# State-space loop: two of the four turned products of each block move from VectorE to GpSimd

## The reference, cut to what matters

```python
def _s5_mixer(h, ...):
    bu_re = einsum('bsgc,gpc->bsgp', u, bb_re)     # the inputs of the states
    bu_im = einsum('bsgc,gpc->bsgp', u, bb_im)
    h_re, h_im = scan over s of  h = a * h + bu    # complex, 64 groups x 64 states
    y = (einsum('bsgp,gcp->bsgc', h_re, c_re) - einsum('bsgp,gcp->bsgc', h_im, c_im) + d * u)
    act = gelu(y)
    zg = act @ glu_w + glu_b
    return zg[..., :D_MODEL] * sigmoid(zg[..., D_MODEL:])
```

## Time and profile before

| | |
|---|---|
| median of 3 runs | 878.67 us (875.8 to 879.58) |
| the profiled execution | 876.96 us, of which the span of the profile is 875.2 us |
| TensorE busy | 804.0 us, 92% of the span |
| VectorE busy | 326.0 us, 37% |
| GpSimd busy | 183.1 us, 21% |
| ScalarE busy | 189.6 us, 22% |
| the state-space loop | from about 435 to 506 us of the span |

### The profile page before, as it was taken

The page is one execution under the profiler, slowest core; times in us unless marked ns, Lnnn a source line. Parts: engine busy times, 40 slices in busy tenths (PEclk is TensorE's granted clock), DMA queues, the critical chain, the costliest instruction groups (busy, mean ns, idle before and its releaser), DMA issues.

```text
span 875.2 us, 12777 instructions
## 1 busy us (share of the span) xinstructions
PE 804.0 (92%) x5191; PEld 449.3 (51%) x5192; DVE 326.0 (37%) x740; ACT 189.6 (22%) x315; POOL 183.1 (21%) x285
## 2 busy tenths in 40 slices
PE   3899979999999999999679999769999999989894
PEld 1367634565465565554555554434444756535441
DVE  1437994461131131311599711342000313214224
ACT  2402330351231221311700110421001203101112
POOL 2518679029400000000123200040011112101000
PEclk9999999999999999999979999869999999999998
DMA  9999999949999999994997792502788799999992
GB/s 322 347 357 387 382 369 342 345 158 422 420 421 422 422 423 422 422 420 204 363 372 264 259 382 97 192 17 100 294 318 304 274 422 417 419 420 420 418 401 76
DMA packets 72263, 289.66 MB, mean 331 GB/s; under 512 B 9302, under 2 KB 10614, under 8 KB 47384
## 3 DMA queue, kind: packets, MB, share of 16 engines
q1 hardware_dynamic: 66784, 279.98, 82.0%
q0 software_dynamic: 4736, 7.35, 2.5%
q10 hardware_dynamic: 696, 1.68, 0.5%
HBM read 281.64 MB, written 13.63 MB: 337 GB/s over the span
## 4 chain that ended last, share of the span: by engine, by line
PE 80%; DMA 9%; DVE 7%; SPq 2%; ACT 1%; issue 1%; DVEq 0%; ACTq 0%
PE PS L1876 20%; PE PS L1897 13%; PE PS L1905 7%; PE PS L2247 7%; PE PS L1879 6%; DMA ring<-in_moe_w 6%; PE PS L1929 4%; PE PS L1834 3%; PE PS L1608 3%; PE PS L1638 3%; DMA ring<-in_ab_w_in 2%; PE PS L1700 2%; PE PS L2232 2%; PE PS L1717 2%; SPq L392 2%; PE PS L2210 1%
## 5 line engine op out<-in xcount | busy, mean ns | idle before, releaser
L1897 PE MATMUL PS<-ring,work 128*64 128x512 f32 (+1 forms) x512 | 129.3, 595 | 2.6 <-DMA ring<-in_moe_w 2.5
L1876 PE MATMUL PS<-ring,hT 128*64 128x256 f32 x896 | 109.2, 386 | 7.4 <-DMA ring<-in_moe_w 7.4
L1876 PE MATMUL PS<-ring,yg 128*64 128x256 f32 x896 | 106.2, 379 | 0.0
L1425 DVE TENSOR_TENSOR work<-work,PS 128x512 f32<-128x512 f32 x32 | 22.0, 688 | 208.2 <-PE PS L1876 158.8
L1876 PEld LDWEIGHTS PS<-ring,hT 128*64 128x64 f32 x896 | 62.7, 138 | 49.1 <-issue 11.8
L1897 PEld LDWEIGHTS PS<-ring,work 128*64 128x64 f32 (+1 forms) x512 | 42.8, 143 | 76.0 <-issue 69.5
L1876 PEld LDWEIGHTS PS<-ring,yg 128*64 128x64 f32 x896 | 64.5, 137 | 32.6 <-issue 0.4
L1905 PE MATMUL PS<-work,xhat 128*128 128x256 f32 (+1 forms) x256 | 66.0, 417 | 4.0 <-issue 4.0
L682 POOL DMA_INDIRECT y_rows<-yg,row_no x24 | 23.4, 974 | 188.4 <-DVE yg L1433 164.9
L1905 PEld LDWEIGHTS PS<-work,xhat 128*128 128x128 f32 x256 | 48.9, 193 | 24.3 <-issue 18.3
L2247 PE MATMUL PS<-ring,yg 128*128 128x512 f32 x128 | 59.4, 615 | 0.0
(11 more groups left out here) (410 smaller groups left out, 1025.7 us busy)
## 6 DMA issues: line engine op xcount, KB each, us to landing
ring<-in_moe_w SPq DMA_DIRECT2D x96, 2048.0 KB, 16.0
ring<-in_ada_w SPq DMA_DIRECT2D x20, 2048.0 KB, 16.1
work<-in_ada_w SPq DMA_DIRECT2D x4, 2048.0 KB, 14.0
ring<-in_s_glu_w SPq DMA_DIRECT2D x4, 2048.0 KB, 11.8
ring<-in_ab_w_in SPq DMA_DIRECT2D x3, 2048.0 KB, 22.1
ring<-in_ab_w_out SPq DMA_DIRECT2D x2, 2048.0 KB, 15.4
ring<-rot_tables SPq DMA_DIRECT2D x2, 2048.0 KB, 11.2
rot_tables<-grow POOLq DMA_DIRECT2D x8, 256.0 KB, 5.6
```

Of the source, the lines that this page charges most:

```text
L1425: v.tensor_tensor(pairs_out(he[:, e % 2, :]), pairs_out(he[:, e % 2, :]), pairs(bank[e % 2 * 2 + 1 if direct else 1]), ALU.mult).then_inc( ...
L1876: last = mm(dst[64 * u:64 * u + 64, 0:256], hg[k][:, e * P:e * P + 64], w[:, k, 256 * u:256 * u + 256], start=k == 0, stop=k == KD - 1)
L1897: last = mm(dst, left[:, at:at + (64 if narrow else P)], w[:, c4, h * HALF:(h + 1) * HALF], start=c4 == 0, stop=c4 == KF - 1)
```

## The change

GpSimd makes products 0 and 3 of `turned(k)`, VectorE products 1 and 2, for every block. GpSimd's order becomes `turned(0)`, `sums(1)`, and then `sums(k + 1)`, `turned(k)`. The sums no longer wait for `q_ready` of the block before. All of GpSimd's steps in the loop count on one semaphore, `pool_s5`; `SUMMED(k)` and `TURNED(k)` are its values after the sums and the turned products of block `k`. `q_ready` now rises twice per block, after the scans and after VectorE's own products. In `products(k)` VectorE makes products 0 and 2 first and then waits for GpSimd's `turned(k - 2)`, whose operands products 1 and 3 overwrite. TensorE's `outputs(k)` and SP's two loads wait for both engines.

```diff
--- before.py
+++ after.py
@@ -67,6 +67,8 @@
 ADA_FIRST = 4
 ADA_EARLY = 16
 ADA_ALL = 24
+SUMMED = lambda k: max(2 * k - 1, 2)
+TURNED = lambda k: min(2 * k + 2, 2 * KD - 1) if k else 1
 SH_M, SC_M, G_M, SH_F, SC_F, G_F = range(6)
 
 
@@ -469,7 +471,8 @@
                             for jj, q in enumerate((0, 2)):
                                 send(GLU_BASE + jj, glu[:, :, q * HALF:(q + 1) * HALF], HALF, HALF)
                     for jj, q in ((2, 1), (3, 3)):
-                        sp_.wait_ge(S("q_ready"), KD // 2 if jj == 2 else KD)
+                        sp_.wait_ge(S("q_ready"), KD if jj == 2 else 2 * KD)
+                        sp_.wait_ge(S("pool_s5"), TURNED(KD // 2 - 1 if jj == 2 else KD - 1))
                         send(GLU_BASE + jj, glu[:, :, q * HALF:(q + 1) * HALF], HALF, HALF)
             for b in range(NB):
                 sp_.wait_ge(S("out_ready"), b + 1)
@@ -637,12 +640,28 @@
             pool.wait_ge(S("x_new"), 2)
             for q in range(4):
                 pool.dma_start(glub[q], a["s5_glu_b"][0].rearrange("(r n) -> r n", r=4)).then_inc(S("glub_in"), 16)
-            for k in range(1, KD):
+            def sums(k):
+
                 p_ = pr[k % 2]
                 pool.wait_ge(S("s_used"), k + 1)
-                pool.wait_ge(S("q_ready"), k)
                 g.tensor_tensor(p_[0], p_[0], p_[1], ALU.add)
-                g.tensor_tensor(p_[2], p_[2], p_[3], ALU.subtract).then_inc(S("sum_ready"), 1)
+                g.tensor_tensor(p_[2], p_[2], p_[3], ALU.subtract).then_inc(S("pool_s5"), 1)
+
+            def turned(k):
+
+                m = k % 2
+                pool.wait_ge(S("q_ready"), 2 * k + 1)
+                if k >= 2:
+                    pool.wait_ge(S("y5_ps"), k - 1)
+                g.tensor_tensor(qq[m][:, 0, :], pr[m][1], rot[:, k, 0, :], ALU.mult)
+                g.tensor_tensor(qq[m][:, 3, :], pr[m][3], rot[:, k, 0, :], ALU.mult).then_inc(S("pool_s5"), 1)
+
+            turned(0)
+            sums(1)
+            for k in range(1, KD):
+                if k + 1 < KD:
+                    sums(k + 1)
+                turned(k)
             def clear_rows():
 
                 pool.wait_ge(S("gates_ready"), 1)
@@ -1547,8 +1566,10 @@
                     dve.wait_ge(S(f"rot_in{k // 4}"), 16)
                 dve.wait_ge(S("s5_ps"), k + 1)
                 v.tensor_tensor(f4(p_[0]), bre, f4(c_), ALU.mult)
+                v.tensor_tensor(f4(p_[2]), bim, f4(c_), ALU.mult)
+                if k >= 2:
+                    dve.wait_ge(S("pool_s5"), TURNED(k - 2))
                 v.tensor_tensor(f4(p_[1]), bim, f4(s_), ALU.mult)
-                v.tensor_tensor(f4(p_[2]), bim, f4(c_), ALU.mult)
                 v.tensor_tensor(f4(p_[3]), bre, f4(s_), ALU.mult).then_inc(S("s_used"), 1)
 
             def scans(k):
@@ -1558,7 +1579,8 @@
                         r_ = s5c[:, 0, 4 * k + q4:4 * k + q4 + 1].to_broadcast([P, NJ])
                         last = v.tensor_tensor_scan(pr[k % 2][2 * w + 1][:, q4 * NJ:(q4 + 1) * NJ], r_,
                                                     pr[k % 2][2 * w][:, q4 * NJ:(q4 + 1) * NJ], 0.0, ALU.mult, ALU.add)
-                link(last)
+                last.then_inc(S("q_ready"), 1)
+                dve.wait_ge(S("q_ready"), 2 * k + 1)
 
             def turned(k):
 
@@ -1567,11 +1589,9 @@
                 gg = (pr[m][1], pr[m][3])
                 if k >= 2:
                     dve.wait_ge(S("y5_ps"), k - 1)
-                v.tensor_tensor(qq[m][:, 0, :], gg[0], c_, ALU.mult)
                 v.scalar_tensor_tensor(qq[m][:, 1, :], gg[1], -1.0, s_, ALU.mult, ALU.mult)
-                v.tensor_tensor(qq[m][:, 2, :], gg[0], s_, ALU.mult)
-                v.tensor_tensor(qq[m][:, 3, :], gg[1], c_, ALU.mult).then_inc(S("q_ready"), 1)
-                dve.wait_ge(S("q_ready"), k + 1)
+                v.tensor_tensor(qq[m][:, 2, :], gg[0], s_, ALU.mult).then_inc(S("q_ready"), 1)
+                dve.wait_ge(S("q_ready"), 2 * k + 2)
 
             products(0)
             dve.wait_ge(S("s_used"), 1)
@@ -1583,7 +1603,7 @@
             for k in range(1, KD):
                 if k + 1 < KD:
                     products(k + 1)
-                dve.wait_ge(S("sum_ready"), k)
+                dve.wait_ge(S("pool_s5"), SUMMED(k))
                 scans(k)
                 turned(k)
             mod_evac(2)
@@ -2223,7 +2243,8 @@
                     pe.wait_ge(S("k0_evac"), 2)
                 mm(dst[:, 0:T], diagD[:, m, :], hT[:, k, :].rearrange("p (j l) -> p l j", l=2), start=True, stop=False)
                 mm(dst[:, 0:NJ], K0[:, k, :], hT[:, k, 0::2], start=False, stop=False)
-                pe.wait_ge(S("q_ready"), k + 1)
+                pe.wait_ge(S("q_ready"), 2 * k + 2)
+                pe.wait_ge(S("pool_s5"), TURNED(k))
                 for w in range(4):
                     for l, tab in ((1, H1), (0, H0)):
                         n = NJ - 1 + l
```

## The result

| | before | changed |
|---|---|---|
| median | 878.23 us (875.8 to 879.58, 6 runs) | 890.5 us (887.21 to 893.05, 6 runs) |
| profiled execution | 876.96 us, span 875.2 | 888.54 us, span 886.7 |

The ratio is 1.0141, with a 95% interval from 1.0114 to 1.0168: the change made the kernel slower by 12 us. The forecast was 896 us, its range 884 to 906.

The account below looks back on a forecast made before the run. TensorE was taken as the bound at 7.45 us a block, the VectorE and GpSimd pair after the change at 10.35; 876.96 + 16.5 (`outputs(6)` later) + 1.7 (clock) = 895.2, with half the median offset 896 us, range 884 to 906.

Parts of the forecast that it names:

- The bound before: State-space loop before the change: TensorE sets the pace at 7.45 us a block, so a faster VectorE buys nothing.
- The collision: Loop: VectorE instructions with two SBUF operands and GpSimd ones reading SBUF exclude each other, each GpSimd instruction costing 1.27 us.
- rival B: Loop: only `turned` collides, scans escape through their broadcast column; cycle 7.85 us, 879 to 881 us; chance 0.09.
- rival A: Loop: no exclusion, turned products and scans overlap freely; cycle 6.65 us, 877 to 879 us, no change; chance 0.06.
- The cycle of 10.35 us: Loop, VectorE and GpSimd per block: 0.15 + 1.25 + 5.15 + 3.75, plus 0.05 for VectorE's own wait.
- The alternation: Loop: the engines take turns; if VectorE's second turned product stands through both of GpSimd's, the cycle is 11.55 us, giving 903.
- The start: First blocks, from `scans(0)` ending at 441.51: `products(2)` done about 449.7, GpSimd's `turned(1)` at 458.6, TensorE stalling from there.
- E(1): Time at which GpSimd ends `turned(1)` in the loop, forecast at 458.6; `outputs(1)` began at 455.25 before.
- The shift of `outputs(6)`: TensorE, late in the loop: `outputs(6)` begins at 510.45 instead of 493.92, 16.5 us later, and the delay stays.
- The clock: TensorE's matmuls at `outputs(6)`: after 4.15 us of idling the clock falls to 1.2 GHz, costing 1.7 us once.
- Rival C: Loop: clock falls in every hole and stays down, TensorE's block near 14.5 us; 914, a mixture 905 and up; chance 0.06.
- The sum: Whole run: 876.96 + 16.5 + 1.7 = 895.2 us profiled; half of a 1.7 us median offset added, giving 896.

Follow-up runs that it names:

- the memset run: Changed kernel with GpSimd's sums and turned products replaced by memsets to the same places, all waits kept; 878.31 us, ratio 1.0011 to the kernel before.
- no overlap: Changed kernel, GpSimd doing turned(k) then sums(k + 1), sums again waiting for `q_ready`, its turned products starting only after VectorE's own; 887.41 us, ratio 1.0099.
- the extra memset: Changed kernel plus one GpSimd memset of 1024 columns, result unused, ahead of each block's sums; 891.15 us, ratio 1.0146 to the kernel before.

## Why the prediction was right

- **The bound before.** TensorE sets the pace: right, and shown by the memset run, in which VectorE is lighter, waits 1.10 us a block for TensorE, and the time is 1.0011 of before.
- **The collision.** Right in every pair foreseen: scans with sums, turned with turned, and none with `products`. The broadcast column did not save the scans (rival B), and rival A fell with it.
- **The cycle of 10.35 us** was 9.54. Taken from one end of GpSimd's `turned` to the next (467.51 to 477.04), the terms were: 1.30 us to the start of the scans, where 0.15 + 1.25 were forecast; 4.71 for scans and sums, where 5.15 were; 3.52 for `turned` with its handover, where 3.75 were. The 0.05 for VectorE's own wait did not appear. The largest error is the price of a collision: it costs VectorE 1.04 us (4.70 less 2.63 is 2.07 for two), and not the 1.25 that I took from GpSimd's whole duration; the earlier trace rows had shown 1.13 as the lower value. The end of GpSimd's `turned` falls together with the end of VectorE's first two `products` (467.51 and 467.70), so the new wait costs VectorE nothing: it has no hole in the block.
- **The alternation.** Strict, one for one, in every block; the 11.55 us case did not come. At 107.07 VectorE stood still through two GpSimd instructions; why it did there and not in the loop is open.
- **The start.** E(1) was 457.96, less the 0.96 us from before the loop 457.0, against 458.6. Of these 1.6 us, 0.9 lie ahead of `scans(1)` (449.72 less 0.96 is 448.8, against 449.7): only one of VectorE's two first turned products was lengthened. The rest is again the price of the collisions.
- **The shift of `outputs(6)`.** 16.5 us predicted, 10.9 measured: five blocks of 0.8 us less are 4.1, the start 1.6. After it the 10.02 us of TensorE and the 27.68 us of the GLU stay as forecast.
- **The clock.** I counted 1.7 us for a fall before `outputs(6)`, from a hole of 4.15 us. With the shorter cycle the hole was 3.27 us; in the profiled execution the clock did not fall there, and the matmuls took 1.95. Of the eight variants seven have a hole at this place. In six of these the matmuls were slower: 3.61 and 3.63 us after holes of 4.03 and 4.30 (copy and product in front of the sums), 3.61 after 3.25 (memset), 3.31 after 3.85 (one product moved), 3.34 after 2.78 (no overlap) and 2.73 after 2.41 (sums back beside `products`). In the seventh, with only the sums moved, they took 1.95 after 3.39. In the changed kernel it happened once in `outputs`, at `outputs(4)`, after a hole of only 2.02 us; there it cost nothing, since `outputs(5)` still waited 0.38 us for GpSimd. TensorE's timeline of the changed kernel at `outputs(4)` first, then that of the variant with the extra memset at `outputs(6)`, and the stretch of the latter, whose granted clock is 0.53:

```profile
486.72 3.58 PE L2253 MATMUL PS<-work 128*32 128x128 f32 x64 [2.02 <-POOL work L657]
```

```profile
507.36 3.61 PE L2256 MATMUL PS<-work 128*32 128x128 f32 x64 [3.25 <-POOL work L660]
```

```profile
507.36:510.97 3.61, 3.61 (x68) 3.56 (x72) 3.58 (x10) 0.00 (x0) 1.19 (x1) 0.53 0.02 5
```

  So the term belongs to some executions and not to others, and holes of equal length went both ways: 2.02 us stand before `outputs(4)` in the variant with the memset too, and there the matmuls took 1.95. Taking it as certain was wrong. Whether it is in the median is open: the six runs of the changed kernel go from 887.21 us at a mean clock of 0.965 to 893.05 at 0.956, but the kernel before, which has no such hole, also spreads over 3.8 us, and the mean clock covers the whole span. Rival C, a clock that falls in every hole and stays down, did not come: the matmuls of seven of the eight `outputs` took 1.95 us.
- **The sum.** 895.2 us were forecast for the profiled execution, 888.54 came, 6.7 less: 5.6 in the shift of `outputs(6)` and 1.7 for the clock, less the 0.6 us that stay of the late start of the loop. The median then lies 2.0 us above this execution, where I had added 0.8. The upper bound of the forecast, 903, was added up wrongly: its terms give 902.

What was mis-sized is thus the price of a collision, with it the cycle (0.8 us a block too long) and the start, and the 1.7 us of the clock that this execution did not have. The mechanism held. All these errors go one way. Against them stand only the 0.6 us of the late start and 1.2 us more between the median and the profiled execution, which the forecast did not foresee, so 896 lies 5.5 us above the result.

## What to carry to other kernels

Before moving elementwise work from VectorE to GpSimd, list for each GpSimd instruction that reads SBUF which VectorE instructions lie beside it and how many SBUF operands these read: with one, nothing was lengthened here, with two nearly the whole GpSimd instruction was added (1.04 us of 1.27), while the product moved away was worth 0.61. An old wait that looks superfluous may be what keeps two engines apart: dropping one line made this kernel 1.7% slower. And find in the timeline which engine has no holes before relieving its neighbour.

## What was not expected of the hardware

The collision works the same for a one-operand GpSimd copy (1.10 us long, scans longer by 0.78), and not at all for a memset, even of twice the columns. GpSimd itself pays little when it meets short scans: its sums grew from 1.27 to 1.33 and 1.40 us, where beside a 512-column product it paid 0.5. One scan of 128 columns takes 0.33 us, so it may be that it stands behind one short scan only; this was not tested. And a hole of TensorE of 2.02 us was followed by the lower clock (granted 0.52 while the matmuls ran) where one of 3.27 us in the same execution was not (1.00).
